# Mix stage and up-projection in one block: operand loads, differences and splits inside the last mix tiles; rows loaded ahead of weight pieces in the down-projection

## The chip, the core and the metric

The kernel runs on one core of one Trainium2 chip. The metric is the device time of one execution in microseconds (us); smaller is better. All data is float32. Matrix products are made as three products of a high and a low part (hi*hi, hi*lo, lo*hi), where the high part is the operand rounded to the type of TensorE's fast float32 mode and the low part is the remainder.

## What is computed

One layer of a streaming encoder over 2048 tokens of width 1024, cut to what matters:

```
h    = layer_norm(x)
q, k, v, u = split(h @ w_in)
mix  = concat([attention(q, k, v), conformer_conv(u)]) @ w_o
h1   = layer_norm(alpha * h + mix)
z    = causal_conv3(h1 @ w_up)                 # 2 * 2816 channels
act  = gelu(z[:, :2816]) * z[:, 2816:]
out  = layer_norm(alpha * h1 + act @ w_down)
```

## The kernel before

There are three stages, one after the other. Each is a block: every engine runs its own list of instructions, ordered by semaphores that are written out by hand, and the next block starts when all engines are through.

**Projection** (`phase_project`) is not touched.

**Mix stage** (`phase_mix`). 16 tiles of 128 tokens go through a software pipeline of five positions, `body(q, p, c, n, m)`: m is rotated and its convolution summed, n has its scores and softmax, c is projected with `w_o`, p gets its residual and layer norm, q is transposed and stored. Three more bodies drain the pipeline after tile 15 has been n (tiles count from 0). On VectorE (DVE) a body begins with `residual(p)` and ends with `row_norm(p)`: three one-column instructions (lines 111, 113, 115) and a `tensor_scalar` over the row (L1096). `affine(p)` on GpSimd (POOL) then multiplies by the gain and adds the bias (L877, L879). TensorE (PE) may write the projection of c into `m_y` only when `residual` of the tile before has read it (`after(pe, resid_ok, c.t)` in `project_attn`). `residual(p)` also waits until the row of two tiles before has left its buffer `m_r` (`h1_st`). The normed rows go to memory as rows (L770) and transposed (L774), both through SyncE's (SP) DMA queue, which also carries all loads.

**Feed-forward stage** (`phase_ffn`). The up-projection is Strassen's scheme in the Winograd form: 1024 tokens at a time (pass p), seven products of half-size operands, `Q1 Q6 Q7 Q5 Q2 Q4 Q3`. A step makes one pair of 128-channel tiles for 1024 tokens: seven products of 12 matmuls. The right operands are the quarters of the transposed rows, B11, B12, B21, B22, and their differences T1 = B12 - B11, T2 = B22 - T1, T3 = T2 - B11, T4 = B21 - T2. They are loaded from memory into `u_stage` and `u_gy` (L1569), cast to the high part on ScalarE (ACT, `right_hi`, L1726) and subtracted to the low part on DVE (`right_lo`, L1873), once per pass. In `first`, the differences of pass 0 are made on DVE (L1965, L1970, L1972, L1975). The left operands are loaded per step (L1565), summed on POOL (L1648 to L1654) and split on ACT (L1716) and DVE (L1869).

The down-projection is the same scheme again: 7 phases of 8 units, 33 matmuls each (L2307). Unit u needs 128 token rows of the gated product, loaded by `load_rows(u)`, cast by `rows_hi` (ACT, L1517) and split by `rows_lo` (DVE, L1533). During phase ph the weights of phase ph+1 are prepared in 11 pieces, two per unit in the first four (`SHARE`): `load_piece`, `weight_sum` (POOL, L1507 and L1509), `piece_hi` (ACT, L1529), `piece_lo` (DVE, L1538). Five buffers `d_wd_raw` go round. On ACT, unit u does in this order: `rows_hi(u+1)` (not for u = 0), `take(u-1)`, then the pieces of its share; DVE likewise.

Of the kernel before, what the change touches and what calls it, by code (L numbers as in the profile page):

```python
# [22 lines left out]
F32 = mybir.dt.float32  # L23
# [597 lines left out]
def phase_mix(nc, trig_scr, par, con, w_o, ln_g, ln_b, h_scr, qkv_scr, conv_scr, h1_scr, h1T_scr):  # L621
    ctx = ExitStack()
    with ctx:
        def sb(name, shape, dt=F32):
            return ctx.enter_context(nc.sbuf_tensor(name, shape, dt))

        def ps(name, shape):
            return ctx.enter_context(nc.psum_tensor(name, shape, F32))

        used = []  # L630

        def sem(name):
            used.append(ctx.enter_context(nc.semaphore(name)))
            return used[-1]

        wo_hi = sb("m_wo_hi", [P, KT, D], F32R)
        wo_lo = sb("m_wo_lo", [P, KT, D], F32R)
        mix_hi = sb("m_mix_hi", [P, 2, KT, P], F32R)
        mix_lo = sb("m_mix_lo", [P, 2, KT, P], F32R)
        ident, ones = sb("m_ident", [P, P]), sb("m_ones", [P, P])  # L640
        turned = sb("m_turned", [P, 2, 5, P])
        eps, one = sb("m_eps", [P, 1]), sb("m_one", [P, 1])
        cg, cb, sink = sb("m_cg", [P, CT]), sb("m_cb", [P, CT]), sb("m_sink", [P, NKV, GROUPS])
        g_bc, b_bc = sb("m_g", [P, D]), sb("m_b", [P, D])
        cos, sin = sb("m_cos", [P, SEQ]), sb("m_sin", [P, SEQ])
        wo_raw = sb("m_wo_raw", [P, WO_SLOTS, D])
        qk_in = sb("m_qk_in", [P, 2, 5, P])
        v_in = sb("m_v_in", [P, 2, CHUNK + P])
        conv_in = sb("m_conv_in", [P, 2, CT, P])
        h_in = sb("m_h_in", [P, 2, D])  # L650
        qk_cos, qk_sin = sb("m_qk_cos", [P, 5, P]), sb("m_qk_sin", [P, 5, P])
        qr, kr = sb("m_qr", [P, CHUNKS, 4 * CHUNK]), sb("m_kr", [P, CHUNK + P])
        vw = sb("m_vw", [P, CHUNKS, P])
        prob = sb("m_prob", [P, NKV, GROUPS, KEYS + 1])
        top, peak = sb("m_top", [P, NKV, GROUPS]), sb("m_peak", [P, NKV, GROUPS])
# [46 lines left out]
        block = ctx.enter_context(nc.Block())  # L702

        q_rows = qkv_scr.rearrange("q p t -> (q p) t")
        half = ROT // 2

        def load_wo(eng, k):

# [1672 lines left out]
```

## Time and profile before

| what | us |
|---|---|
| median of 3 runs | 2026.48 |
| lowest, highest | 2026.16, 2028.93 |
| the profiled execution, its own time | 2024.93 |
| its span, first to last instruction | 2023.2 |
| PE busy | 1871.2 |
| DVE busy | 1555.3 |
| ACT busy, POOL busy | 977.7, 961.6 |

PE is the busiest engine with 92% of the span; the mean granted clock of TensorE over the span is 0.968 of full speed. Times in the rows count from the start of the span. A timeline row gives start, duration, engine, line, operation, output<-input, shapes, count, and in brackets the idle time of the engine before it and what ended it.

### The profile page before, as it was taken

The page shows a single profiled execution, that of the slowest core. Times are in us where ns is not written, and L with a number is a line of the kernel's source. Part 1 is how long each engine was busy: PE and PEld are TensorE (multiplying, and loading weights), DVE is VectorE, ACT ScalarE, POOL GpSimd, SP SyncE. Part 2 cuts the span into 40 slices and gives each one's busy share as a digit, 9 for nine tenths or more (in the row PEclk, how much of TensorE's full clock was granted, in tenths as well). Part 3 has the DMA queues.
Part 4 walks back from the last instruction along what each step waited for, and adds up shares of the span by engine and source line. Part 5 has one row for each costly group of instructions (what it writes and reads, how often), then busy time and mean ns, then how long its engine had stood idle before and what let it go on. Part 6 is the DMA issues. An engine that isn't in the chain of part 4 may idle for free.

```text
span 2023.2 us, 27605 instructions
## 1 busy us (share of the span) xinstructions
PE 1871.2 (92%) x8520; PEld 1528.4 (76%) x8520; DVE 1555.3 (77%) x1874; ACT 977.7 (48%) x1508; POOL 961.6 (48%) x694
## 2 busy tenths in 40 slices
PE   3899999489999489999999899999999799999997
PEld 3788888367777368888888678888888688788886
DVE  8779878479998488888878888888888644666786
ACT  4555556367777344444444544444444333232454
POOL 5587788246666335444444554444443555520000
PEclk8999999699999699999999999999999899999999
DMA  7311211634443432322322332222224544387553
GB/s 253 146 36 64 71 57 47 195 108 149 139 144 106 170 124 96 120 95 97 116 93 102 109 108 101 104 105 102 104 104 143 173 130 147 122 276 237 176 185 137
DMA packets 200043, 257.48 MB, mean 127 GB/s; under 512 B 12208, under 2 KB 131504, under 8 KB 199472
## 3 DMA queue, kind: packets, MB, share of 16 engines
q1 hardware_dynamic: 191456, 233.24, 35.2%
q10 hardware_dynamic: 8528, 23.51, 3.2%
q8 instruction: 30, 0.49, 0.1%
q14 instruction: 29, 0.24, 0.0%
HBM read 172.10 MB, written 84.61 MB: 127 GB/s over the span
## 4 chain that ended last, share of the span: by engine, by line
PE 35%; issue 14%; POOL 8%; DVE 4%; DMA 3%; ACT 1%; SPq 0%; POOLq 0%; ACTq 0%; DVEq 0%
PE u_mm L2078 19%; PE d_y L2307 16%; DMA d_wd_raw<-w_down 2%; POOL u_w_sum L1650 1%; POOL u_w_sum L1648 1%; DVE u_r_lo L1873 1%; POOL d_wd_raw L1509 1%; POOL u_s L1664 1%; POOL u_s L1667 1%; DVE d_a_lo L1533 1%; POOL d_wd_raw L1507 1%; POOL u_s L1661 1%; DVE u_w_lo L1869 1%; ACT d_a_hi L1517 0%; DMA d_a_raw<-gated_scr 0%
## 5 line engine op out<-in xcount | busy, mean ns | idle before, releaser
L2078 PE MATMUL u_mm<-u_r_hi,u_w_hi 128*128 128x512 f32 x1232 | 484.0, 393 | 42.1 <-DVE u_r_lo L1873 26.2
L2078 PE MATMUL u_mm<-u_r_lo,u_w_hi 128*128 128x512 f32 x1232 | 482.3, 391 | 0.0
L2078 PE MATMUL u_mm<-u_r_hi,u_w_lo 128*128 128x512 f32 x1232 | 482.2, 391 | 0.0
L2078 PEld LDWEIGHTS u_mm<-u_r_hi,u_w_hi 128*128 128x128 f32 x1232 | 233.2, 189 | 95.3 <-issue 39.8
L2078 PEld LDWEIGHTS u_mm<-u_r_lo,u_w_hi 128*128 128x128 f32 x1232 | 233.4, 189 | 48.5
L2078 PEld LDWEIGHTS u_mm<-u_r_hi,u_w_lo 128*128 128x128 f32 x1232 | 233.0, 189 | 48.7
L2307 PE MATMUL d_y<-d_wd_hi,d_a_hi 128*128 128x512 f32 x616 | 243.4, 395 | 14.3 <-DVE d_a_lo L1533 13.9
L2307 PE MATMUL d_y<-d_wd_lo,d_a_hi 128*128 128x512 f32 x616 | 242.2, 393 | 0.0
L2307 PE MATMUL d_y<-d_wd_hi,d_a_lo 128*128 128x512 f32 x616 | 241.9, 393 | 0.0
L1904 DVE SCALAR_TENSOR_TENSOR u_y<-u_z,u_taps,u_y 128x1024 f32<-128x1024 f32 x176 | 222.6, 1287 | 15.1 <-DVE u_z L1918 3.5
L524 DVE SCALAR_TENSOR_TENSOR a_acc<-a_glu,a_taps,a_acc 128x2048 f32<-128x2048 f32 x84 | 197.9, 2356 | 15.2 <-DVE a_acc L524 14.4
L1648 POOL TENSOR_TENSOR u_w_sum<-u_w_raw 128x512 f32<-128x512 f32 x44 | 58.9, 1339 | 305.3 <-DMA u_w_raw<-w_up 286.5
L1869 DVE TENSOR_TENSOR u_w_lo<-u_w_raw,u_w_hi 128x512 fp32r<-128x512 f32 x132 | 147.3, 1117 | 43.3 <-ACT u_w_hi L1716 43.2
L545 PE MATMUL a_mm<-a_hT_hi,a_w_hi 128*128 128x512 f32 (+1 forms) x448 | 176.6, 394 | 0.0
L413 POOL TENSOR_TENSOR a_gb<-a_gb,a_spare 128x512 f32<-128x512 f32 x128 | 161.3, 1309 | 30.9 <-ACT a_spare L311 30.9
L545 PE MATMUL a_mm<-a_hT_hi,a_w_lo 128*128 128x512 f32 (+1 forms) x448 | 175.4, 391 | 0.0
L545 PE MATMUL a_mm<-a_hT_lo,a_w_hi 128*128 128x512 f32 (+1 forms) x448 | 175.3, 391 | 0.0
L1716 ACT CAST u_w_hi<-u_w_sum 128x512 fp32r<-128x512 f32 x176 | 105.1, 620 | 111.9 <-POOL u_w_sum L1650 44.2
L2307 PEld LDWEIGHTS d_y<-d_wd_hi,d_a_hi 128*128 128x128 f32 x616 | 117.1, 190 | 41.5 <-DVE d_a_lo L1533 15.6
L1869 DVE TENSOR_TENSOR u_w_lo<-u_w_sum,u_w_hi 128x512 fp32r<-128x512 f32 x176 | 137.9, 793 | 9.2 <-ACT u_w_hi L1716 3.7
L2307 PEld LDWEIGHTS d_y<-d_wd_hi,d_a_lo 128*128 128x128 f32 x616 | 117.2, 190 | 24.7
L2307 PEld LDWEIGHTS d_y<-d_wd_lo,d_a_hi 128*128 128x128 f32 x616 | 117.3, 190 | 24.4
(214 smaller groups left out, 3420.5 us busy)
## 6 DMA issues: line engine op xcount, KB each, us to landing
u_w_raw<-w_up SPq DMA_DIRECT2D x44, 1024.0 KB, 5.0
d_a_raw<-gated_scr SPq DMA_DIRECT2D x56, 704.0 KB, 5.1
gated_scr<-u_s SPq DMA_DIRECT2D x88, 256.0 KB, 2.0
d_wd_raw<-w_down SPq DMA_DIRECT2D x88, 256.0 KB, 5.1
gated_scr<-u_gy SPq DMA_DIRECT2D x44, 256.0 KB, 2.1
a_xs<-x SPq DMA_DIRECT2D x16, 512.0 KB, 4.6
m_h_in<-h_scr SPq DMA_DIRECT2D x16, 512.0 KB, 4.0
h_scr<-m_r SPq DMA_DIRECT2D x16, 512.0 KB, 4.7
```

Of the source, the lines that this page charges most:

```text
L413: nc.gpsimd.tensor_tensor(p, p, prod[:, i % 2, :], ALU.add).then_inc(part_ok, 1)
L524: v = nc.vector.scalar_tensor_tensor(out=acc[:], in0=src, scalar=tap_of(j, k), in1=acc[:], op0=ALU.mult, op1=ALU.add)
L545: last = nc.tensor.matmul(mm[bank][:], w[:, slot, k, :], h[:, k, rhs_at], start=(k == 0 and w is w_hi and h is hT_hi), stop=(k == KT - 1 a ...
L1507: nc.gpsimd.tensor_tensor(t, t, wd_hi[:, old, k, :].bitcast(F32), ALU.subtract).then_inc(wsum_ok, 1)
L1509: nc.gpsimd.tensor_tensor(t, t, wd_lo[:, old, k, :].bitcast(F32), ALU.subtract).then_inc(wfin_ok, 1)
L1533: nc.vector.tensor_tensor(a_lo[:, u % 2, :, :], a_raw[:, u % 2, :, :], a_hi[:, u % 2, :, :].bitcast(F32), ALU.subtract).then_inc(alo_ok, 1)
L1648: nc.gpsimd.tensor_tensor(w_sum[:, 0, :, :], a21, raw_of(Q4), ALU.add).then_inc(sum_ok, 1)
L1716: nc.scalar.copy(w_hi[:, s, :, :], left_of(s)).then_inc(whi_ok, 1)
L1869: nc.vector.tensor_tensor(w_lo[:, s, :, :], left_of(s), w_hi[:, s, :, :].bitcast(F32), ALU.subtract).then_inc(wlo_ok, 1)
L1904: v = nc.vector.scalar_tensor_tensor(out=y[:, m, :], in0=z[:, m, k:k + SPAN], scalar=tap(st, m, k), in1=y[:, m, :], op0=ALU.mult, op1=ALU.add)
L2078: last = nc.tensor.matmul(mm[BANK[s]][:], w[:, s, k, :], h[:, s, k, :], start=(s in FRESH and k == 0 and w is w_hi and h is r_hi), stop=(k ...
L2307: m = nc.tensor.matmul(dy[u % BANKS][:], a[:, u % 2, k, :], w[:, ph % 2, k, :], start=(k == 0 and a is a_hi and w is wd_hi), stop=(k == HA ...
```

## The change

`phase_mix` and `phase_ffn` become one function and one block, `phase_rest`. No engine meets another between the two stages any more, and the semaphores of the mix stage are not cleared in between. All buffers of the up-projection are laid over those of the mix stage in an order that lets them be written as the mix buffers die: the form of Q1 and Q6 lie over those parts of the `w_o` operands that tile 15's `project_rest` reads last, Q7 and Q5 over the rest, Q2 over the mix operands, Q4 over `m_h_in` and the gain, Q3 over `m_r` and `m_h1T`. Each engine's list goes on past tile 15:

- SP issues the four 1 MB loads of pass 0's operands, the taps and the bias between the bodies of tile 12 and tile 13, the first left operand after tile 14's body, B22 a second time after two more bodies, and the second left operand after the last transposed row is stored.
- POOL makes three left sums, then T1, T2 and T3 (2048 columns each) right after its body of tile 15.
- DVE and ACT mix the splits of the seven right operands and of the first left operands with the residuals, norms and copies of tiles 14 and 15. `row_norm` of tiles 13, 14 and 15 applies gain and bias itself (two `scalar_tensor_tensor` of 1024 columns on DVE), and POOL's `affine` is left out for them.
- PE makes Q1, Q6, then transposes row tile 14, then Q7, Q5, Q2, transposes row tile 15, then Q4, Q3.

In the down-projection the rows of unit 3 and two more weight pieces are loaded before the last store of the up-projection, the casts and splits of a phase's pieces begin one unit later (`SHARE[i - 1]` in unit i), and `take` of units 0 and 1 has new waits, because `d_total` now lies elsewhere. High and low part of the down weights share one buffer.

The core of the diff:

```diff
+            sp.wait_ge(wo_lo_ok, KT)
+            for s in range(2):
+                sp.wait_ge(h1T_st[s], 16 * (NT // 4 + 1))
+            load_b(stage[:, 0, :, :], 0, 0, 0, b11_ld)
+            load_b(stage[:, 1, :, :], 0, 0, 1, b12_ld)
+            load_b(stage[:, 2, :, :], 0, 1, 1, b22_ld)
+            load_b(spare, 0, 1, 0, b21_ld)
+            sp.dma_start(taps[:, :, :], ...).then_inc(con_ld, 16)
+            sp.dma_start(bias[:], ...).then_inc(con_ld, 16)
+            for t in (NT - 3, NT - 2):
+                body(at(t - 3), at(t - 2), at(t), at(t + 2), at(t + 3))
+            sp.wait_ge(cos_ok, NT)
+            sp.wait_ge(sin_qk_ok, 2 * NT)
+            load_w(0)
...
+            left_sums(Step(0, 0, 0), 3)                       # POOL, after body of tile 15
+            nc.gpsimd.tensor_tensor(stage[:, 1, :, :], stage[:, 1, :, :], stage[:, 0, :, :], ALU.subtract).then_inc(diff_ok, 1)
+            nc.gpsimd.tensor_tensor(stage[:, 2, :, :], stage[:, 2, :, :], stage[:, 1, :, :], ALU.subtract).then_inc(diff_ok, 1)
+            nc.gpsimd.tensor_tensor(early, stage[:, 2, :, :]..., stage[:, 0, :, :]..., ALU.subtract).then_inc(diff_ok, 1)
...
+            residual(c)                                       # DVE, c is tile 14, d is tile 15
+            log_gate(d)
+            attn_lo(d)
+            weights_lo(opening, Q1)
+            swish(d)
+            conv_lo(d)
+            row_stats(c)
+            weights_lo(opening, Q6)
+            weights_lo(opening, Q7)
+            row_norm(c)
+            for s in (Q5, Q2, Q4):
+                weights_lo(opening, s)
+            right_lo(0, Q1)
+            right_lo(0, Q6)
+            residual(d)
+            right_lo(0, Q7)
+            row_stats(d)
+            right_lo(0, Q5)
+            make_u2(opening)
+            row_norm(d)
+            make_u3(opening)
+            right_lo(0, Q2)
+            make_c22(opening)
+            nc.vector.tensor_tensor(spare, spare, stage[:, 2, :, :], ALU.subtract).then_inc(t4_ok, 1)
+            weights_lo(opening, Q3)
+            right_lo(0, Q4)
+            make_c21(opening)
+            for s in range(2):
+                dve.wait_ge(h1T_st[s], 16 * (NT // 2 + 1))
+            right_lo(0, Q3)
...
+            product(opening, Q1, 0)                           # PE
+            product(opening, Q6, 0)
+            turn_rows(c)
+            product(opening, Q7, 0)
+            product(opening, Q5, 0)
+            product(opening, Q2, 0)
+            turn_rows(d)
+            product(opening, Q4, 0)
+            product(opening, Q3, 0)
...
-                if ph < P3:
-                    for k in SHARE[i]:
+                if ph < P3 and i:
+                    for k in SHARE[i - 1]:
                         piece_hi(act, ph + 1, k)
...
+                    if u == 0:
+                        act.wait_ge(act_ok, 2 * FT)
+                    if u == 1:
+                        act.wait_ge(odd_st, 32 * FT)
+                        act.wait_ge(s4_ok, FT)
                     nc.scalar.copy(total[:, LO, i, FIRST], dy[u % BANKS][:]).then_inc(dp1_ok, 1)
```

## Rows read from the trace of the kernel before

**Rows 1.** The page, part 2: tenths of PE busy in 40 slices, clock below.

```profile
PE   3899999489999489999999899999999799999997
PEclk8999999699999699999999999999999899999999
```

**Rows 2.** Busy time by stretch: start:end, length, PE, PEld, DVE, ACT, POOL, PEclk, DMA.

```profile
655.00:667.00 12.00, 11.93 (x56) 9.76 (x56) 5.11 (x12) 2.56 (x6) 3.90 (x2) 1.00 0.26 89
667.00:697.00 30.00, 3.22 (x17) 2.45 (x17) 7.80 (x12) 8.59 (x11) 11.21 (x7) 0.56 0.58 205
697.00:733.20 36.20, 23.77 (x85) 18.16 (x86) 31.84 (x24) 15.63 (x16) 10.04 (x5) 0.85 0.23 83
752.40:771.50 19.10, 19.10 (x86) 15.83 (x85) 16.50 (x19) 8.87 (x13) 14.53 (x9) 1.00 0.27 97
```

**Rows 3.** Timeline of PE at the boundary of the two stages.

```profile
655.07 0.73 PE L1245 MATMUL m_y<-m_wo_hi,m_mix_hi 128*128 128x512 f32 x2 [1.21 <-ACT m_mix_hi L927]
697.01 0.77 PE L2078 MATMUL u_mm<-u_r_hi,u_w_hi 128*128 128x512 f32 x1 [16.77 <-DVE u_r_lo L1873]
```

**Rows 4.** Timeline of PE in the down-projection: the three stalls and the spacing after one.

```profile
1593.22 0.80 PE L2307 MATMUL d_y<-d_wd_hi,d_a_hi 128*128 128x512 f32 x1 [5.88 <-DVE d_a_lo L1533]
1597.22 0.63 PE L2307 MATMUL d_y<-d_wd_hi,d_a_hi 128*128 128x512 f32 x1
1598.51 0.63 PE L2307 MATMUL d_y<-d_wd_hi,d_a_hi 128*128 128x512 f32 x1
1608.06 0.79 PE L2307 MATMUL d_y<-d_wd_hi,d_a_hi 128*128 128x512 f32 x1 [4.36 <-DVE d_a_lo L1533]
1741.69 0.50 PE L2307 MATMUL d_y<-d_wd_hi,d_a_hi 128*128 128x512 f32 x1 [3.38 <-DVE d_a_lo L1533]
```

**Rows 5.** Timeline of DVE and POOL around the last mix tiles.

```profile
620.19 0.81 DVE L1096 TENSOR_SCALAR m_r<-m_r,m_mv,m_l 128x1024 f32<-128x1024 f32 x1
649.51 0.15 DVE L1088 TENSOR_SCALAR m_l<-m_mv 128x1 f32<-128x1 f32 x1
652.78 1.22 DVE L1056 SCALAR_TENSOR_TENSOR m_r<-m_h_in,m_y 128x1024 f32<-128x1024 f32 x1 [1.22 <-PE m_y L1245]
694.57 2.29 DVE L1873 TENSOR_TENSOR u_r_lo<-u_stage,u_r_hi 128x2048 fp32r<-128x2048 f32 x1 [2.77 <-ACT u_r_hi L1726]
643.52 0.46 POOL L873 TENSOR_TENSOR m_square_sum<-m_square_pair 128x128 f32<-128x128 f32 x1
```

**Rows 6.** Timeline of POOL and DVE where both read SBUF; line 113: min/median/max ns.

```profile
1116.62 4.63 POOL L1691 TENSOR_TENSOR u_stage<-u_stage 128x2048 f32<-128x2048 f32 x1 [1.32 <-DVE u_edge L1916]
1120.17 3.22 DVE L1873 TENSOR_TENSOR u_r_lo<-u_stage,u_r_hi 128x2048 fp32r<-128x2048 f32 x1 [1.21 <-ACT u_r_hi L1726]
L113 DVE SCALAR_TENSOR_TENSOR m_l<-m_l x16: 159/1214/1223, 440.6 to 672.2; 128x1 f32<-128x1 f32 x16
```

**Rows 7.** Timeline of SP's queue and of DVE where the loads go in.

```profile
610.25 0.42 SPq L770 DMA_DIRECT2D h_scr<-m_r  x1
621.05 1.22 DVE L1056 SCALAR_TENSOR_TENSOR m_r<-m_h_in,m_y 128x1024 f32<-128x1024 f32 x1
685.44 0.46 SPq L1569 DMA_DIRECT2D u_stage<-h1T_scr  x1
691.89 0.60 SPq L1604 DMA_DIRECT2D u_bias<-par  x1
```

**Rows 8.** DMA issues between 684 and 705: count, KB each, median us to landing.

```profile
u_stage<-h1T_scr SPq DMA_DIRECT2D x3, 1024.0 KB, 11.5
u_w_raw<-w_up SPq DMA_DIRECT2D x1, 1024.0 KB, 4.9
u_bias<-par SPq DMA_DIRECT2D x1, 22.0 KB, 9.3
```

**Rows 9.** Timeline of ACT between the first units of the down-projection.

```profile
1587.04 1.14 ACT L1529 CAST d_wd_hi<-d_wd_raw 128x512 fp32r<-128x512 f32 x2
1588.09 1.36 ACT L1517 CAST d_a_hi<-d_a_raw 128x1408 fp32r<-128x1408 f32 x1
```

More of the change, by code:

```diff
@@ L829, in _, with step @@
+            def step(st):
+                left_sums(st.plus(1))
+                gated_sums(st.plus(-1))
             for s in range(2):
@@ new lines, in final @@
+            def final(st):
+                prev = st.plus(-1)
+                weights_hi(st, Q3)
+                tap_g(prev)
+                keep_p1(st)
+                gelu(prev)
+                act.wait_ge(mm_ok, made(st, Q6))
+                rows_hi(act, 0)
+                act.wait_ge(mm_ok, made(st, Q7))
+                rows_hi(act, 1)
+                for k in range(5):
+                    piece_hi(act, P1, k)
+                take_c11(st)
+                for k in range(5, HALF):
+                    piece_hi(act, P1, k)
+                tap_v(st)
+                tap_g(st)
+                gelu(st)
@@ new lines, in _ @@
+            out_T(d)
+            act.wait_ge(h1_st[1], 16 * (NT // 2 + 1))
+            act.wait_ge(h1_st[0], 16 * (NT // 2 + 1))
+            right_hi(0, Q3)
+            for s in (Q1, Q6, Q7, Q5, Q2, Q4):
+                weights_hi(opening.plus(1), s)
+            tap_v(opening)
+            step(Step(0, 1, 0))
+            with act.Fori(1, HALF - 1) as n:
+                step(Step(n, 0, 0))
+                step(Step(n, 1, 0))
+            step(Step(HALF - 1, 0, 0))
+            turn(Step(HALF - 1, 1, 0))
@@ L1204, in _, with product @@
+            turn(Step(HALF - 1, 1, 0))
+            again(Step(HALF, 0, 1))
+            with dve.Fori(HALF, FT - 1) as n:
+                step(Step(n, 1, 1))
+                step(Step(n, 2, 1))
+            final(Step(FT - 1, 1, 1))
         @block.tensor
         def _(pe):
+            def product(st, s, fresh):
+                pe.wait_ge(wlo_ok, split(st, s))
+                if fresh is not None:
+                    pe.wait_ge(rlo_ok, 7 * fresh + FORMS[fresh].index(s) + 1)
+                if s in FRESH:
+                    after(pe, {Q1: c11_ok, Q6: u2_ok, Q7: c21_ok, Q5: c12_ok}[s], st.i)
+                else:
+                    pe.wait_ge({Q2: p1_ok, Q4: u3_ok, Q3: c22_ok}[s], st.i + 1)
+                for k in range(HK):
+                    for w, part in ((w_hi, HI_PART), (w_hi, LO_PART), (w_lo, HI_PART)):
+                        last = nc.tensor.matmul(mm[BANK[s]][:], w[:, s, k, :], forms[:, POS[s], part, k, :],
+                                                start=(s in FRESH and k == 0 and w is w_hi and part == HI_PART),
+                                                stop=(k == HK - 1 and w is w_lo), skip_group_check=s not in FRESH)
+                last.then_inc(mm_ok, 1)
@@ L1206, in _, with step @@
+            def step(st, fresh=None):
+                for s in st.order():
+                    product(st, s, fresh)
             pe.wait_ge(con_ld, 16 * 5)
@@ L2274, in _ @@
                     rows_lo(dve, u + 1)
-                if ph < P3:
-                    for k in SHARE[i]:
+                if ph < P3 and i:
+                    for k in SHARE[i - 1]:
                         piece_lo(dve, ph + 1, k)
```

1482 lines of the change are left out of this document (713 added, 769 removed).

## The prediction, made before the changed kernel was built or run

> **What bounds the kernel now.** I read the page's slices first: PE is full nearly everywhere, and the granted clock is full (2.4 GHz) except at three dips [rows 1]. So only places where PE stands still, or restarts at the low clock, can give anything. The busy time by stretch then shows the boundary of the two stages. The last `w_o` product ends at 667.1; in the 30 us after it PE is busy 3.2, at a granted clock of 0.56, and in the next 36.2 us, which hold the first step of the up-projection, it is busy 23.8, at 0.85. A later step takes 19.1 us with PE full [rows 2]. The timeline of PE shows Q1 starting at 697.01, released by the low part of its right operand [rows 3]. So 66.1 us pass between the last mix product and the second step (733.2), where 19.1 us of products and under 2 us of transposes are needed: about 45 us could be won at most. The third view is DVE in the same place: it is busy 31.8 of the 36.2 us [rows 2]. The opening is bound by DVE's splits and differences as much as by the loads ahead of them. The fourth is PE in the down-projection: three stalls of 5.9, 4.4 and 3.4 us, all released by `rows_lo` [rows 4].
>
> **The opening, if nothing held the engines up.** Until tile 15's products begin, everything stands as before. After them DVE has to do, in order, 8 instructions of 2048 columns (seven low parts and T4), 15 of 512 columns, a residual, two sets of statistics and two norms. With 2.21 us for each long one (the row's 2.29 less the overlap of neighbours [rows 5]), 0.6 for a short one, 1.2 for a residual, 1.8 for statistics and 3.0 for a norm with gain and bias, that is 17.7 + 9.0 + 1.2 + 3.6 + 6.0 = 37.5 us, where each long part also needs 1.8 us of ACT ahead of it. I laid the lists of all engines out with these durations. Q1 then starts at 668.7, the last low part (Q3's, which waits for tile 15's transposed row to land) ends about 697.5, and step 2 starts at 702.8: 30.3 us earlier than 733.2.
>
> **What POOL adds.** The differences T1 to T3 move from DVE to POOL, at 4.6 us each instead of 2.2 [rows 6], and they stand right before the moment at which DVE norms tile 13. The trace shows what that does. A split of 2.2 us that began at 1120.17 took 3.22, ending 2.1 us after POOL's 4.63 us difference had ended (1121.25): it waited for POOL. The one-column instruction L113 takes 159 ns alone and 1214 ns in the median of 16, whenever POOL adds two buffers at that moment [rows 6]. So a DVE instruction that reads SBUF as POOL does waits for the end of POOL's instruction, and where both wait, one DVE instruction slips in between two of POOL's. The Trainium skill says the same (SBUF — State Buffer, Who interferes with whom: an exclusive lock, and the second one to issue fully blocks). By that rule the change is hurt here, and the trace agrees with it.
>
> Priced: POOL ends its sums of tile 15 at 643.98 [rows 5], three left sums of 1.3 bring it to 647.9, three differences to 652.5, 657.2 and 662.1. DVE starts tile 13's variance at 649.51 [rows 5]; its norm is five locking instructions, of which one passes at 652.5 and one at 657.2, so the last three (0.2, 1.2, 1.2) follow at 662.1 and end at 664.7. `residual` of tile 14 stands behind it in DVE's list and ends at 665.9 instead of 654.0. `project_attn` of tile 15 waits for it: PE stands still from 653.9 to 666, restarts at the low clock (+2.5 us), and ends its mix products near 680.7 instead of 667.1. The hand layout gives then: Q1 at 681.3, Q5 done at 693.6, Q2 from 697.4 at the low clock, the last low part at 710.2 (37.5 us of DVE work after 665.9, and 6.8 us of waits for a left sum, for ACT's cast of T4 and for product Q4), Q3 done at 715.3, where step 2 begins; its left operand lands at 713 and its sums are made while Q1 runs. That is 17.8 us earlier than before. A stall of 0.6 us that followed goes too: **-18.4 us**. Bounds: -31 without the blocking, -13 with one more difference in the way.
>
> **What the loads add.** Between tile 12 and 13 SP now issues 4 MB plus taps and bias. The same six issues took 7.0 us from the first (685.44) to the end of the last (691.89 + 0.60) [rows 7]. Their data came in order: the left operand issued first landed in 4.9 us, the 22 KB of bias, issued last, took 9.3 [rows 8], to 701.2. Tile 10's row store, before issued at 610.25, comes at about 617 now, behind these loads: 4 MB from 609.7 at the 390 GB/s of that stretch, then 0.5 MB of tile 13's input, then the row, about 625. `residual` of tile 12, at 621.05 before [rows 7], waits for that store: 4 us late, and PE is full there, so the delay goes through. After its 4 us, PE may restart at the low clock (+2). Bounds: 0, if the store isn't held by the loads ahead of it, and +7. I take **+5 us**.
>
> The norms of the last tiles cost DVE 2.4 us instead of the 0.81 of L1096 [rows 5]; for tile 13 this is in the layout above, and POOL's 4.8 us per tile fall away on the path from norm to transpose (in the layout too). Clearing of semaphores, the meeting of the engines and the new table load (1.3 us, on ACT behind tile 14's copy) cost nothing beyond the layout: DVE's splits cover them, and if they did not, they would cost 1.3.
>
> **Down-projection.** Unit 2 began at 1593.22 after 5.88 us of standing still, because ACT did two weight pieces (1587.04) before `rows_hi(2)` (1588.09), and DVE likewise [rows 9]. With the pieces one unit later, `rows_hi(2)` comes at 1587.0, its split ends at 1590 or, behind a POOL sum, 1591.2, and unit 2 begins 2.5 us earlier. The restart still falls to 1.2 GHz: after the stall three matmuls took 1.29 us (1597.22 to 1598.51) [rows 4], 0.43 each against 0.228 (19.1/84 [rows 2]), and that kept for a dozen matmuls: 2.3 us. Unit 2 then ends at about 1600.6. The rows of unit 3 are loaded already and cast before pieces 2 and 3, so they are ready at 1594 and the stall of 4.36 goes with its restart (2.3). Unit 3 would end at 1608.1; before, it began at 1608.06 and ended at 1617.8: 9.7 us. The third stall (3.38 at 1741.69, and 1.5 for its restart) comes from rows waiting behind pieces that POOL hasn't summed; with pieces loaded one unit ahead of use ACT doesn't wait for them: 4.9 us. `take(1)` waits for the last store to land (about 1591), before anything needs its bank. The price of the longer hold of the five buffers is that SP's loads wait for the splits of the unit before, which two units of lead cover; without that cover a stall like the old ones comes back. Sum: **-14.6 us**, bounds -5 (only the first two shrink) and -17.
>
> **Sum.** -18.4 + 5 - 14.6 = -28.0 us. The profiled execution took 2024.93 us (span 2023.2, 1.7 around it), 1.5 below the median. Against its own time that gives 1996.9; against the median of 2026.48, 1998.5 us.
>
> **Rivals.**
> - *The lock costs little, or the loads do not hold the row store.* If DVE's norm of tile 13 passes between POOL's instructions, the opening brings 31 instead of 18.4: 1986; if the loads cost nothing as well, 1981. For it: a DVE instruction whose operand lies in PSUM is not held (residuals, copies of z), and most of the tail's short instructions are of that kind. Against: the norm's five all read SBUF.
> - *New waits in the tail and a smaller gain below.* The loads cost 7, one more wait on ACT (in-order casts, T4) costs 5, and in the down-projection only the first stalls shrink (-8): -18.4 + 5 + 7 - 8 = -14.4, so 2012. For it: every engine's list is now one chain through the tail, and DVE is at its limit there.
> - *Slower: TensorE stays at 1.2 GHz.* In the stretch between 667 and 697 the granted clock was 0.56 with PE mostly still [rows 2]. The new opening has five stalls of 2 to 12 us within 60 us. If the clock stays low from tile 15's products through the opening and the second step, 11 + 19 + 19 us of products take twice as long, of which 5 are counted above: +44, so 2042. It decides from a mean granted clock under about 0.7 over 650 to 740. Against: every restart in the trace is back at full clock after about 5 us of products.
> - *It does nothing.* If some engine still had to wait for all others (DVE's wait for tile 15's transposed row stands before the last split only), the opening would stay as it is, and the loads' 5 us would take part of the gain below: -10, 2016. Not likely.
>
> **Chances.** Forecast (1993 to 2006): 0.55. First rival (1980 to 1992): 0.22. Second (2007 to 2016): 0.13, the idle one 0.03. Slower: 0.04. The rest, within 0.2% of before, 0.03. The range 1982 to 2011 leaves out less than 2 in 10. A difference of 0.2% (4 us) is about what a measurement of this kernel can tell from none. Faster by more than that: 0.93; within: 0.03; slower: 0.04.
>
> **What would show it.** In the trace after: POOL's three 4.6 us instructions end near 662 plus the delay of the loads; the two `scalar_tensor_tensor` of tile 13 follow them and not the statistics; PE stands still for about 12 us before `project_attn` of tile 15; Q1 starts 9 to 13 us before its old 697.0 (15.7 earlier, less what the loads cost); no unit of the down-projection but the third waits over 1 us. If PE goes on into tile 15's products without a stall, the lock was priced wrongly; if `residual` of tile 12 begins on time, the loads were.

## The result, and the profile after

The changed kernel takes 2009.47 us in the median of 4 runs (2007.70 to 2010.80); the kernel before took 2026.32 us beside it (4 runs, 2025.25 to 2028.93). The ratio is 0.9919, 95% interval 0.9906 to 0.9931: 16.8 us faster, 0.8%. The forecast was 1998.5 us, or 28 us faster. The sign and the range 1982 to 2011 held, but 11 us of the gain are missing: the time lies outside the 1993 to 2006 that the prediction gave to its own account (0.55) and inside the 2007 to 2016 of its second rival (0.13). The profiled execution of the changed kernel, the slowest of the four, took 2010.80 us with a span of 2007.8 us, 15.4 less than the span before.

The page, part 2, of the changed kernel, tenths of PE busy in 40 slices and the clock below, to be read beside [rows 1]:

```profile
PE   4899999489999689999999799999999899989997
PEclk9999999689999889999999999999999999999999
```

The 4 of the fourteenth slice has become a 6, the fifteenth stays at 8, and the 36th falls from 9 to 8. The timeline of PE of the changed kernel names the places (start, us, operation, in brackets the idle time before it and what ended it):

```profile
628.43 1.19 PE L2042 MATMUL m_y<-m_wo_hi,m_mix_hi 128*128 128x512 f32 x2 [4.86 <-DVE m_r L1779]
671.81 1.19 PE L2042 MATMUL m_y<-m_wo_hi,m_mix_hi 128*128 128x512 f32 x2 [11.19 <-DVE m_r L1779]
686.71 0.70 PE L1994 MATMUL u_mm<-u_forms,u_w_hi 128*128 128x512 f32 x2 [0.89 <-DVE u_forms L1617]
715.79 0.70 PE L1994 MATMUL u_mm<-u_forms,u_w_hi 128*128 128x512 f32 x2 [3.03 <-issue]
720.02 0.81 PE L1994 MATMUL u_mm<-u_forms,u_w_hi 128*128 128x512 f32 x2
736.04 0.70 PE L1994 MATMUL u_mm<-u_forms,u_w_hi 128*128 128x512 f32 x2 [2.04 <-DVE u_z L1627]
1125.90 0.69 PE L1994 MATMUL u_mm<-u_forms,u_w_hi 128*128 128x512 f32 x2 [1.05 <-ACT u_z L1327]
1562.16 0.61 PE L2360 MATMUL d_y<-d_wd,d_a_hi 128*128 128x512 f32 x2
1570.66 0.73 PE L2360 MATMUL d_y<-d_wd,d_a_hi 128*128 128x512 f32 x2 [1.53 <-DVE d_wd L898]
1582.99 0.74 PE L2360 MATMUL d_y<-d_wd,d_a_hi 128*128 128x512 f32 x2 [3.88 <-DVE d_a_lo L893]
1782.11 1.22 PE L2360 MATMUL d_y<-d_wd,d_a_hi 128*128 128x512 f32 x2 [2.70 <-DVE d_a_lo L893]
1802.70 0.74 PE L2360 MATMUL d_y<-d_wd,d_a_hi 128*128 128x512 f32 x2 [1.77 <-DVE d_a_lo L893]
```

The first two rows are the two prices that the prediction put on the opening: tile 12's and tile 14's residual come late, and the restart runs at the low clock (two matmuls in 1.19 us; the granted clock was 0.50 in the 2.6 us behind each). Q1 starts at 686.71, 10.3 before its old 697.01 [rows 3]. Q3's twelve matmuls follow at 715.79, and the second step begins at 720.02, 13.2 before 733.20 [rows 2]. Then comes a stall that the prediction did not have (736.04, granted clock 0.68 in the 5.3 us behind it), and three in the fourth phase of the down-projection (1782 to 1803), where the kernel before ran full. Of the down-projection's old stalls [rows 4] only unit 2's is left, 3.88 instead of 5.88; unit 3 and unit 20 wait no more. Within unit 0 there is a new one of 1.53.

For the places in between, four rows of the kernel before: PE at the first pass's last step, PE at unit 0, and DVE taking the products of units 24 and 30:

```profile
1135.76 0.47 PE L2078 MATMUL u_mm<-u_r_hi,u_w_hi 128*128 128x512 f32 x1 [1.06 <-ACT u_z L1737]
1571.15 0.39 PE L2307 MATMUL d_y<-d_wd_hi,d_a_hi 128*128 128x512 f32 x1
1781.03 0.69 DVE L2215 TENSOR_TENSOR d_total<-d_total,d_y 128x512 f32<-128x512 f32 x1 [0.61 <-PE d_y L2307]
1825.91 0.69 DVE L2215 TENSOR_TENSOR d_total<-d_total,d_y 128x512 f32<-128x512 f32 x1 [1.28 <-PE d_y L2307]
```

and the last two in the changed kernel:

```profile
1757.00 0.69 DVE L2268 TENSOR_TENSOR d_total<-d_total,d_y 128x512 f32<-128x512 f32 x1 [4.39 <-PE d_y L2360]
1810.56 0.69 DVE L2268 TENSOR_TENSOR d_total<-d_total,d_y 128x512 f32<-128x512 f32 x1 [2.43 <-PE d_y L2360]
```

How far the changed kernel is ahead at each place, and what the prediction's sum gives there:

| place | before | after | ahead | predicted |
|---|---|---|---|---|
| second step begins | 733.20 | 720.02 | 13.2 | 12.8 |
| last step of the first pass | 1135.76 | 1125.90 | 9.9 | 13.4 |
| unit 0 | 1571.15 | 1562.16 | 9.0 | 13.4 |
| unit 24 taken | 1781.03 | 1757.00 | 24.0 | 28.0 |
| unit 30 taken | 1825.91 | 1810.56 | 15.4 | 28.0 |
| end of the span | 2023.2 | 2007.8 | 15.4 | 28.0 |

So the two large terms came as predicted: the opening with its loads (13.2 for 12.8) and the down-projection up to unit 24 (24.0 - 9.0 = 15.0 for 14.6). Each row compares one execution with one: at 600 us, where the two kernels still do the same, the changed one is already 0.7 us late (a transposed row is issued at 600.62 for 599.94), so differences under 1 us say little. The missing 12.6 us of span went in two places: between the second step and unit 0, where 0.6 more should have been won and 4.2 were lost, and in the fourth phase of the down-projection, where 8.7 were lost (24.0 to 15.4). Twice 0.4 go the other way.

**The new stall in the second step.** Timeline of SP, ACT and DVE of the changed kernel:

```profile
712.52 0.38 SPq L967 DMA_DIRECT2D u_w_raw<-w_up  x1
717.38 0.62 ACT L1303 CAST u_w_hi<-u_w_raw 128x512 fp32r<-128x512 f32 x1 [6.43 <-DMA u_w_raw<-w_up]
727.19 5.12 DVE L1648 SCALAR_TENSOR_TENSOR u_y<-u_z,u_taps,u_y 128x1024 f32<-128x1024 f32 x4
```

SP issues the second step's left operand only when all stores of the mix stage have landed, at 712.52. ACT stands still for 6.43 us for it, DVE splits it up to 727 and only then begins the four taps of the first step. `make_u2` and `make_u3`, which add up PE's products, stand behind them, and PE waits for the second.

**The new stalls in the fourth phase.** Timeline of SP and DVE of the changed kernel:

```profile
1763.86 9.00 SPq L853 DMA_DIRECT2D d_wd_raw<-w_down  x4
1772.90 0.91 SPq L2154 DMA_DIRECT2D d_h<-h_scr  x2
1772.08 0.68 DVE L2268 TENSOR_TENSOR d_total<-d_total,d_y 128x512 f32<-128x512 f32 x1
1779.29 1.22 DVE L2271 SCALAR_TENSOR_TENSOR d_total<-d_h,d_total 128x1024 f32<-128x1024 f32 x1 [6.54 <-DMA d_h<-h_scr]
```

SP's four issues of weight pieces take 9.00 us, because each waits for one of the five piece buffers (in the kernel before, four such issues took 3.81). The two loads of h1 stand behind them on SP and go out at 1772.90. DVE needs h1 at 1772.76, waits 6.54 us, and `rows_lo` of the next unit stands behind it and runs from 1780.43, so PE waits too. The same place in the kernel before, where the pieces were split one unit earlier:

```profile
1790.48 0.80 SPq L2106 DMA_DIRECT2D d_h<-h_scr  x2
1796.71 1.22 DVE L2218 SCALAR_TENSOR_TENSOR d_total<-d_h,d_total 128x1024 f32<-128x1024 f32 x1
```

There h1 is issued 6.2 us before DVE uses it, and nothing waits.

### The profile page after: what moved, and what is told of

It reads as the page before. It is cut to its first block, busy times and chain, and to the rows that moved or that the text cites. A ratio compares the mean times of both kernels' runs of the same rounds, so it can differ in the third digit from the quotient of the medians.

```text
span 2007.8 us, 27606 instructions
## 1 busy us (share of the span) xinstructions
PE 1871.0 (93%) x8520; PEld 1529.7 (76%) x8520; DVE 1572.8 (78%) x1874; ACT 975.4 (49%) x1508; POOL 968.3 (48%) x691
## 4 chain that ended last, share of the span: by engine, by line
PE 38%; issue 17%; DVE 11%; POOL 6%; ACT 3%; DMA 3%; SPq 1%; POOLq 0%; ACTq 0%; DVEq 0%
PE u_mm L1994 19%; PE d_y L2360 18%; POOL u_w_sum L1146 1%; POOL u_w_sum L1144 1%; DMA d_h<-h_scr 1%; POOL u_s L1164 1%; DVE u_w_lo L1608 1%; POOL u_s L1167 1%; DVE u_forms L1617 1%; DVE m_stat L1806 1%; POOL u_s L1161 1%; ACT m_ce L1481 1%; DVE m_top L1837 1%; PE m_y L2042 1%; DVE m_den L1850 1%
## 5 line engine op out<-in xcount | busy, mean ns | idle before, releaser
L1994 PE MATMUL u_mm<-u_forms,u_w_hi 128*128 128x512 f32 x2464 | 767.1, 393 | 24.2 <-issue 12.1
L1994 PEld LDWEIGHTS u_mm<-u_forms,u_w_hi 128*128 128x128 f32 x2464 | 466.3, 190 | 125.4 <-issue 22.3
L1994 PE MATMUL u_mm<-u_forms,u_w_lo 128*128 128x512 f32 x1232 | 483.0, 392 | 0.0
L2360 PE MATMUL d_y<-d_wd,d_a_hi 128*128 128x512 f32 x1232 | 382.5, 392 | 11.7 <-DVE d_a_lo L893 10.1
L2360 PEld LDWEIGHTS d_y<-d_wd,d_a_hi 128*128 128x128 f32 x1232 | 232.4, 189 | 62.4 <-DVE d_a_lo L893 11.8
L1994 PEld LDWEIGHTS u_mm<-u_forms,u_w_lo 128*128 128x128 f32 x1232 | 233.5, 190 | 49.2
L2360 PE MATMUL d_y<-d_wd,d_a_lo 128*128 128x512 f32 x616 | 240.7, 391 | 0.0
L893 DVE TENSOR_TENSOR d_a_lo<-d_a_raw,d_a_hi 128x1408 fp32r<-128x1408 f32 x56 | 100.4, 1793 | 46.6 <-ACT d_a_hi L877 46.3
L2360 PEld LDWEIGHTS d_y<-d_wd,d_a_lo 128*128 128x128 f32 x616 | 116.4, 189 | 24.1
L311 ACT ACTIVATE a_spare<-a_glu,a_taps 128x512 f32<-128x512 f32 x128 | 91.9, 724 | 72.1 <-POOL a_gb L413 71.3
```

What stands on the lines that cost most here:

```text
L311: nc.scalar.activation(dst, glu[:, j % 2, bass.ds(c * BLK + k, BLK)], ACT.Copy, scale=tap_of(j, k)).then_inc(prod_ok, 1)
L893: nc.vector.tensor_tensor(a_lo[:, u % 2, :, :], a_raw[:, u % 2, :, :], a_hi[:, u % 2, :, :].bitcast(F32), ALU.subtract).then_inc(alo_ok, 1)
L1994: last = nc.tensor.matmul(mm[BANK[s]][:], w[:, s, k, :], forms[:, POS[s], part, k, :], start=(s in FRESH and k == 0 and w is w_hi and part ...
L2360: m = nc.tensor.matmul(dy[u % BANKS][:], a[:, u % 2, k, :], wd[:, ph % 2, k, part, :], start=(k == 0 and a is a_hi and part == HI_PART), s ...
```

## The experiments

Times are medians; "the changed kernel" is 2009.47 us.

### The six loads behind tile 10's row store

```diff
-            (four load_b, taps, bias)
-            for t in (NT - 3, NT - 2):
-                body(at(t - 3), at(t - 2), at(t), at(t + 2), at(t + 3))
+            t = NT - 3
+            body(at(t - 3), at(t - 2), at(t), at(t + 2), at(t + 3))
+            (four load_b, taps, bias)
+            t = NT - 2
+            body(at(t - 3), at(t - 2), at(t), at(t + 2), at(t + 3))
```

> The changed kernel, but SP issues the four 1 MB loads of the right operand, the taps and the bias after its list for tile 13 (after tile 10's row store) and not ahead of it. Theory (the loads hold the row store, residual of tile 12 waits for it): the stall of 4.86 us of TensorE before tile 12's attention product goes, and with it the restart at the low clock; everything behind it comes 6 to 7 us earlier and stays so: 2002.8 us (2001 to 2005). Rival 1 (the queue has to move these 4 MB anyway, and they now hold tile 11's row store): the stall moves one tile on, 2008 to 2010. Rival 2 (the opening waits for the loads themselves, now later): POOL's first difference starts later than 650.7 + its three left sums, and the time is 2010 to 2014.

Measured: 2003.77 us (2001.55 to 2008.10, 4 runs), ratio to the kernel before 0.9887 [0.9864, 0.9911]; 5.7 less than the changed kernel. Timeline of DVE and PE, first of the changed kernel, then of this one:

```profile
627.06 1.22 DVE L1779 SCALAR_TENSOR_TENSOR m_r<-m_h_in,m_y 128x1024 f32<-128x1024 f32 x1 [5.39 <-DMA h_scr<-m_r]
```

```profile
622.54 1.22 DVE L1781 SCALAR_TENSOR_TENSOR m_r<-m_h_in,m_y 128x1024 f32<-128x1024 f32 x1
666.56 1.19 PE L2044 MATMUL m_y<-m_wo_hi,m_mix_hi 128*128 128x512 f32 x2 [11.21 <-DVE m_r L1781]
```

The wait of 5.39 us for the store is gone, PE's stall of 4.86 us with it, and the stall before tile 15 lies 5.25 us earlier. The loads did hold the row store, and they can be moved without harm: the rivals (the same wait one tile later, or POOL waiting for the operands) did not appear. The time is in the expected range.

### POOL's three differences left out

```diff
-            nc.gpsimd.tensor_tensor(stage[:, 1, :, :], stage[:, 1, :, :], stage[:, 0, :, :], ALU.subtract).then_inc(diff_ok, 1)
+            pool.sem_inc(diff_ok, 1)
```

and likewise for the other two; Q7's form is cast from `stage[:, 2]`. The product of these forms is therefore not the right one; all other work stays.

> The changed kernel without POOL's three differences of the first half (T1 to T3): the forms that need them are cast from the undifferenced buffers, so that part of the result is left out; casts, splits, products and loads stay. Theory (POOL's differences block DVE's norm of tile 13 and so hold residual of tile 14): the stall of 11.19 us before tile 15's attention product goes, to under 1 us, and Q1 of the up-projection comes 11 to 14 us earlier; the stall that DVE's late list causes in the second step stays; 1997 us (1995 to 2001). Rival 1 (DVE is simply behind with its own work there): the stall stays over 5 us, 2004 to 2009. Rival 2 (the gain is won at the stall and given back in the opening, where DVE's splits wait for ACT's casts and for tile 15's transposed row): the stall goes, but the second step begins less than 6 us earlier, 2003 to 2007.

Measured: 1999.83 us (1999.03 to 2002.14, 4 runs), ratio 0.9868 [0.9849, 0.9887]; 9.6 less than the changed kernel. Timeline of PE:

```profile
662.47 0.73 PE L2039 MATMUL m_y<-m_wo_hi,m_mix_hi 128*128 128x512 f32 x2 [1.20 <-ACT m_mix_hi L1444]
677.11 1.19 PE L1991 MATMUL u_mm<-u_forms,u_w_hi 128*128 128x512 f32 x2 [2.57 <-DVE u_forms L1614]
706.16 0.70 PE L1991 MATMUL u_mm<-u_forms,u_w_hi 128*128 128x512 f32 x2 [3.03 <-issue]
```

The stall of 11.19 us is 1.20, Q1 comes 9.6 us earlier, Q3 (706.16 for 715.79) too, and the end as well. So what the differences cost at the stall goes through to the end in full, and none of it is won back in the opening. By itself this run cannot tell POOL's blocking of DVE from the time of the differences; the next one can.

### POOL waits until DVE has normed tile 13

```diff
+            pool.wait_ge(h1_ok, NT - 2)
             pool.wait_ge(b11_ld, 16)
```

> The changed kernel, but POOL starts its first difference only when DVE has ended its norm of tile 13. Theory (what is blocked is DVE work on SBUF alone; residual of tile 14, the gate's log, the low part of the attention and the low part of the convolution read PSUM and pass): the stall of 11.2 us before tile 15's attention product falls under 1.5 us, but DVE's splits and statistics, all in SBUF, now wait for POOL's three differences, so that Q1 starts only 2 to 4 us earlier: 2006 us (2004 to 2008). Rival 1 (instructions with an operand in PSUM are held as well): a stall of 4 to 12 us stays before that product, 2009 to 2012. Rival 2 (POOL's differences hold DVE up nowhere but at the norm): 1998 to 2001, as without them.

Measured: 2003.16 us (2002.51 to 2005.66, 4 runs), ratio 0.9885 [0.9869, 0.9902]; 6.3 less than the changed kernel. Timeline of POOL and DVE:

```profile
660.47 4.60 POOL L1252 TENSOR_TENSOR u_stage<-u_stage 128x2048 f32<-128x2048 f32 x1 [5.57 <-DVE m_r L1828]
665.15 4.94 POOL L1255 TENSOR_TENSOR u_stage<-u_stage 128x2048 f32<-128x2048 f32 x1
660.31 1.21 DVE L1780 SCALAR_TENSOR_TENSOR m_r<-m_h_in,m_y 128x1024 f32<-128x1024 f32 x1
661.61 0.69 DVE L1870 SCALAR_TENSOR_TENSOR m_ce<-m_tps,m_ce 128x512 f32<-128x512 f32 x1
662.82 2.80 DVE L1609 TENSOR_TENSOR u_w_lo<-u_w_raw,u_w_hi 128x512 fp32r<-128x512 f32 x1
667.49 1.28 DVE L1807 BATCH_NORM_STATS2 m_stat<-m_r 128x6 f32<-128x512 f32 x2
669.15 0.15 DVE L1812 TENSOR_SCALAR m_l<-m_mv 128x1 f32<-128x1 f32 x1
```

While POOL's first difference runs (660.47 to 665.07), two DVE instructions with one operand in PSUM (`m_y`, `m_tps`) pass at their usual 1.21 and 0.69 us. The split of `u_w_raw`, both inputs in SBUF, takes 2.80 instead of 0.68 and ends at 665.6. Under the second difference the statistics pass unheld at 1.28 for two, though they read SBUF. So rival 1 is out, the stall is POOL's blocking, and the theory was too wide: what is held is an instruction with two inputs in SBUF, not every one that works there. The stall before tile 15's product is 1.20 us, but PE now waits 9.73 us for Q1's low part, and Q1 comes at 683.98, 2.7 earlier. The gain is larger than expected (2004 to 2008). A part of this is that the second step's stall went too: the left operand is issued at 709.38 instead of 712.52, and DVE begins the taps at 724.20 instead of 727.19. By the last step of the first pass (1122.04) the trace is 3.9 us ahead of the changed kernel's. The rest lies where the edit changes nothing, at units 0 and 2 above all: in the traces of the versions that leave that place alone, unit 0's wait is between nothing and 1.53 us, and unit 2's between 2.77 and 3.88.

### The three differences on DVE

```diff
+            nc.vector.tensor_tensor(stage[:, 1, :, :], stage[:, 1, :, :], stage[:, 0, :, :], ALU.subtract).then_inc(diff_ok, 1)
+            nc.vector.tensor_tensor(stage[:, 2, :, :], stage[:, 2, :, :], stage[:, 1, :, :], ALU.subtract).then_inc(diff_ok, 1)
             right_lo(0, Q1)
+            nc.vector.tensor_tensor(early, ...).then_inc(diff_ok, 1)
             right_lo(0, Q6)
```

and the three on POOL go.

> The changed kernel, but the three differences of the first half are DVE's, 2.2 us each, two ahead of Q1's low part and one ahead of Q6's. Theory (without POOL's differences the kernel took 9.6 us less, and DVE is the bound of the opening, so it pays its 6.6 us there): no stall before tile 15's attention product, the second step starts about 3 us earlier, 2006.5 us (2003 to 2009). Rival 1 (DVE waits for ACT's casts in that place anyway, and the differences fill the gaps): 2000 to 2002. Rival 2 (the differences delay Q1's low part and PE restarts more often): 2009 to 2014.

Measured: 2006.20 us (2001.19 to 2006.73, 4 runs), ratio 0.9897 [0.9881, 0.9914]; 3.3 less than the changed kernel, as its price of 6.6 us on DVE said (9.6 - 6.6 = 3.0). In its trace Q3 starts at 712.25, 3.5 earlier than in the changed kernel. That trace is of the fastest of the four executions; the other three took 2005.7 to 2006.7, and the interval of the ratio lies between 1 and 8 us under the changed kernel's 0.9919.

### The second step's left operand earlier

```diff
-            for t in (NT + 1, NT + 2):
-                body(at(t - 3), at(t - 2), at(t), at(t + 2), at(t + 3))
+            body(at(NT - 2), at(NT - 1), None, None, None)
+            store_row(at(NT - 1))
+            refill(Step(0, 0, 0), 1)
+            store_turned(at(NT - 1))
...
-            refill(Step(0, 0, 0), 1)
```

and ACT waits for tile 15's turned row before `tap_v` of the first step.

> The changed kernel, but SP issues the load of the second step's left operand as soon as its buffer is split (about 706), between tile 15's row store and its transposed store, and not after all stores have landed (712.5). Theory (the left operand lands at 717.4, DVE stands still for it and is then behind in the second step): it lands near 711, and the stall of 2.04 us at 736 goes with its restart: 2005.3 us (2004.5 to 2007). Rival 1 (DVE is behind in the second step because of its own work, the left operand only adds to its idle time): the stall stays, 2009. Rival 2 (the transposed row now lands 2 us later behind the 1 MB, and the last low part and so Q3 waits for it): the second step begins 1 to 2 us later, 2007 to 2010.

Measured: 2005.26 us (2003.53 to 2010.16, 4 runs), ratio 0.9899 [0.9876, 0.9922]; 4.2 less. Timeline of SP, DVE and PE:

```profile
706.44 0.38 SPq L967 DMA_DIRECT2D u_w_raw<-w_up  x1
723.13 5.13 DVE L1650 SCALAR_TENSOR_TENSOR u_y<-u_z,u_taps,u_y 128x1024 f32<-128x1024 f32 x4
716.26 1.19 PE L1996 MATMUL u_mm<-u_forms,u_w_hi 128*128 128x512 f32 x2 [3.03 <-issue]
```

The load goes out 6.1 us earlier, DVE begins the taps 4.1 earlier, and PE then runs without a stall of over 0.5 us until the first pass's last step. Q3 starts at 716.26, 0.5 later than in the changed kernel, but Q1 (687.18 for 686.71) is late by the same 0.5, long before the load goes out, and the wait ahead of Q3 is the same 3.03 us: the store behind the 1 MB cost Q3 nothing, and rival 2 is out. The size of the gain is less sure than its place. The four executions reach from 2003.53 to 2010.16, and the interval of the ratio includes the changed kernel's 0.9919; in the trace 2.3 us are gained by the last step of the first pass (1123.57 for 1125.90).

### h1 ahead of the weight pieces

```diff
+                if ph == P4:
+                    load_h1(i, FIRST, (left_ok, i) if i else None)
                 if 1 < u and ph < P3:
                     for k in SHARE[i]:
                         load_piece(sp, ph + 1, k)
-                if ph == P4:
-                    load_h1(i, FIRST, (left_ok, i) if i else None)
```

> The changed kernel, but in the down-projection's fourth phase SP issues the unit's two loads of h1 ahead of the weight pieces and not behind them. Theory (SP stands at a piece whose buffer is not free yet, h1 is issued late behind it, DVE's take waits for h1 and rows_lo stands behind take): the three stalls of 2.70, 1.77 and 1.77 us at 1782, 1793 and 1803 go, with their restarts: 2002.5 us (2001.5 to 2004). Rival (the queue is full in that phase, 1 MB of pieces, 0.7 MB of rows and 0.5 MB of h1 per 7.5 us): the stalls stay or now wait for the pieces, 2008 to 2011.

Measured: 1999.61 us (1997.45 to 2003.49, 4 runs), ratio 0.9866 [0.9843, 0.9888]; 9.9 less, more than the expected 7 (2001.5 to 2004) and against 8.7 read from the table above. The two traces agree with the 8.7: their spans differ by 9.6, and 0.9 of that is there at unit 24 already, ahead of the edit. Busy time of the stretch 1755 to 1806, first of the changed kernel, then of this one (columns as in [rows 2]):

```profile
1755.00:1806.00 51.00, 44.76 (x188) 35.94 (x187) 24.23 (x27) 14.14 (x16) 10.34 (x9) 0.97 0.69 208
```

```profile
1755.00:1806.00 51.00, 51.00 (x227) 42.24 (x226) 35.97 (x32) 16.25 (x18) 16.86 (x10) 1.00 0.81 251
```

PE is full again, and 251 GB/s are moved where the changed kernel moved 208: the queue had room, SP's order did not use it. The rival is out.

### The down-projection's part alone

The kernel before, with the down-projection's lines of the change and nothing else.

> The kernel before with the change's down-projection part alone: rows of unit 3 and the pieces of the second unit loaded ahead of the turn, and in ACT's and DVE's lists each unit's weight pieces one unit later. Two stages stay apart as before. Theory (the stalls of units 2, 3 and 20 shrink by what the prediction says, 14.6 us, but the longer hold of the five piece buffers makes SP stand ahead of h1 in the fourth phase and gives 7 us back, and unit 0's last piece comes late, 1 to 2 us): 2020 us (2018 to 2022), with three stalls of 1.5 to 3 us in the fourth phase. Rival (the part gains its 14.6 us by itself, and it is the opening that disturbs it in the changed kernel): 2010 to 2014, no stall in the fourth phase.

Measured: 2019.90 us (2018.76 to 2020.64, 5 runs) beside 2026.68 for the kernel before, ratio 0.9964 [0.9950, 0.9978]: 6.8 less. Timeline of PE, the three longest stalls in the down-projection:

```profile
1593.19 0.80 PE L2313 MATMUL d_y<-d_wd_hi,d_a_hi 128*128 128x512 f32 x1 [2.74 <-DVE d_a_lo L1533]
1792.42 0.50 PE L2313 MATMUL d_y<-d_wd_hi,d_a_hi 128*128 128x512 f32 x1 [3.02 <-DVE d_a_lo L1533]
1803.60 0.50 PE L2313 MATMUL d_y<-d_wd_hi,d_a_hi 128*128 128x512 f32 x1 [3.41 <-DVE d_a_lo L1533]
```

The stalls of the fourth phase come with this part, whatever the opening does. The rival, a full 14.6 us from this part, is out. That leaves 10 of the 16.8 us for the stages above. The expectation also had unit 0's last piece late by 1 to 2 us; unit 0 waits 0.18 us here.

### Four mends together

The three single mends above, and ACT's cast and DVE's split of unit 2's rows ahead of the last step's gate.

> The changed kernel with four mends at once: the six loads behind tile 10's row store, the second step's left operand loaded as soon as its buffer is free, h1 ahead of the weight pieces, and, new, ACT's cast and DVE's split of unit 2's rows ahead of the last step's gate (ACT: before the gelu; DVE: after the four taps). Theory (the causes are independent; alone they gave 5.7, 4.2 and 9.9 us, and the last stall before unit 2, 3.88 us with a restart of 2, goes as well): 1985 us (1983 to 1989), stalls left: 11.2 us before tile 15's attention product, the three of the opening and the middle turn. Rival (one gain eats another: with the work earlier the same loads collide elsewhere, or unit 2 then waits for POOL's sums): 1990 to 1998.

Measured: 1989.66 us (1986.82 to 1992.07, 4 runs), ratio 0.9810 [0.9794, 0.9827]; 19.8 less than the changed kernel. That is the sum of the three single ones (5.7 + 4.2 + 9.9 = 19.8); the fourth added nothing that can be seen, and the time is just outside the expected 1983 to 1989, where the rival's range begins. Timeline of ACT and PE:

```profile
1584.67 0.62 ACT L889 CAST d_wd<-d_wd_raw 128x512 fp32r<-128x512 f32 x1 [2.33 <-POOL d_wd_raw L869]
1589.12 0.74 PE L2366 MATMUL d_y<-d_wd,d_a_hi 128*128 128x512 f32 x2 [2.01 <-DVE d_a_lo L893]
```

Unit 2 no longer waits, but unit 4 does, 2.01 us: its rows are cast behind this weight piece in ACT's list, and POOL sums the piece late. PE could take unit 4 at 1587.1, some 14 us earlier than in the changed kernel (about 1601); POOL's first sum behind the last store's operands came only 6.4 earlier (1577.65 for 1584.05). This is the rival's mechanism, two units further on.

### The mended kernel with the differences elsewhere

> The kernel with the four mends, and POOL starts its first difference only when DVE has ended its norm of tile 13. Theory (the gain of 6.3 us that this gave alone is independent of the four, less the 4.2 us that it had in common with the earlier load, since its second step had no stall either): 1986.5 us (1984 to 1989). Rival (with the second step's left operand early, POOL's sums for it block DVE's last low parts): 1989 to 1992.

Measured: 1987.39 us (1984.64 to 1989.87, 5 runs) beside 2025.20 for the kernel before, ratio 0.9812 [0.9798, 0.9827]. The time is in the expected range, but the ratio is that of the four mends without it (0.9810), so a gain from POOL's waiting is not shown here. In the trace the stall of 11.19 us before tile 15's product is 1.20, and PE waits 9.72 us for Q1's low part instead.

> The kernel with the four mends, and the three differences of the first half on DVE, 2.2 us each. Theory (alone this began the second step 2 to 3 us earlier than the version that lets POOL wait, and lost it again at the stall of 2.06 us that the earlier load takes away): 1984.5 us (1982 to 1987), faster than the other by 1 to 4 us. Rival (DVE's own 6.6 us cost as much as POOL's blocking with POOL waiting): equal within 1 us.

Measured: 1984.54 us (1982.92 to 1986.03, 5 runs) beside 2025.20 for the kernel before, ratio 0.9798 [0.9783, 0.9812]: the fastest here, 2% under the kernel before, and as expected. Whether it beats the other one stays open: the medians are 2.9 us apart, but the intervals overlap, and the two profiled spans are 1983.7 and 1983.6 us.

## Why the prediction was right or wrong

**The opening, and POOL in it: right.** The layout, -17.8 of the term's -18.4, is to be read against everything shifted ahead of it. DVE's variance row of tile 13 stands at 656.27 for 649.51 [rows 5], 6.8 later; Q1 was due at 681.3 + 6.8 = 688.1 and came at 686.7; the second step was due at 715.3 + 6.8 = 722.1 and came at 720.0, 2.1 early. (715.3 is 17.9 before 733.20, not 17.8, and the 30.3 of the undisturbed layout is 30.4; nothing hangs on it.) That the opening and the loads together came within 0.4 us (13.2 for 12.8) is in part luck: the opening gave 2.1 more than laid out, the loads took 1.1 more, and 0.7 was lost before either. The blocking went as laid out in kind. Timeline of POOL and DVE of the changed kernel:

```profile
654.58 4.60 POOL L1251 TENSOR_TENSOR u_stage<-u_stage 128x2048 f32<-128x2048 f32 x1
663.88 5.57 POOL L1260 TENSOR_TENSOR u_z<-u_stage 128x2048 f32<-128x2048 f32 x1
656.27 0.15 DVE L1811 TENSOR_SCALAR m_l<-m_mv 128x1 f32<-128x1 f32 x1
659.41 4.37 DVE L115 SCALAR_TENSOR_TENSOR m_l<-m_l 128x1 f32<-128x1 f32 x1
663.82 1.28 DVE L1825 SCALAR_TENSOR_TENSOR m_r<-m_r,m_mv,m_g 128x1024 f32<-128x1024 f32 x1
665.14 5.40 DVE L1827 SCALAR_TENSOR_TENSOR m_r<-m_r,m_l,m_b 128x1024 f32<-128x1024 f32 x1
670.46 1.21 DVE L1779 SCALAR_TENSOR_TENSOR m_r<-m_h_in,m_y 128x1024 f32<-128x1024 f32 x1
```

The one-column `L115` takes 4.37 us. The prediction let one of the norm's five instructions pass each time that POOL changes instruction and had three follow the third difference. In the trace two pass at each change, and only the last of the five waits for the third difference. The residual's end, 671.7, is still within 1 us of 665.9 + 6.8, since the last of the five waits for the third difference either way. PE stood still for 11.19 us where "about 12" was promised. The first rival is out: without the differences the time falls by 9.6 us, and with POOL only made to wait the stall goes. The Trainium skill (SBUF — State Buffer, Who interferes with whom) draws the line at two inputs in SBUF against a GpSimd instruction that reads SBUF, which is narrower than the prediction's rule; the version with POOL waiting agrees, with the split at 2.80 us and the statistics and PSUM readers unheld.

**The loads: right in kind, a little small.** Predicted +5 with bounds 0 and 7. The variance row is 6.8 late, of which 0.7 was there at 600 us, so the loads took 6.1; moved behind the row store they give back 5.7 us of the time. The step that was small is the residual's delay, put at 4: the row was awaited for 5.39 us and PE stood for 4.86, and the restart came on top.

**"A stall of 0.6 us that followed goes too": wrong.** The second step's stall did not go, it became 2.04 us with a restart. The hand layout had the left operand landed at 713 and its sums made while Q1 runs, and left open what DVE's list would do with that: the six splits stand ahead of the first step's taps and of `make_u2`. The landing itself came as laid out: 717.4, that is 2.6 us before the second step began, where the prediction had 2.3 (713 and 715.3). What failed is that so late a landing was taken to be harmless: DVE began the taps 4.1 us later than with the load issued early. In the place of -0.6 stands +3.3 (13.2 to 9.9) by the last step of the first pass; issued early, the load gives 4.2 us in the medians and 2.3 in the trace. Whether `make_u2` ahead of the splits would have done as well was not tried. A second, small loss, 0.9 between 1125.90 and unit 0, falls in the turn between the passes; the version with h1 first, the same up to there, loses 0.2, so most of it is this execution's own.

**The down-projection's gain: right to the place where it had been looked at.** From unit 0 to unit 24 the change gained 15.0 for 14.6. Within it unit 2's part was smaller (1.2 instead of 2.5 earlier against unit 0): PE stopped for 1.53 us at unit 0, for a weight piece that was split late. With h1 first, the same code up to there, unit 0's wait is 0.42 and unit 2 is 2.3 earlier (1582.07, with unit 0 at 1562.33), so the 2.5 nearly holds where that wait is short. Why its length differs from execution to execution is open.

**"SP's loads wait for the splits of the unit before, which two units of lead cover": the step that failed.** It holds for single pieces. In the fourth phase each piece of the next phase is the difference of two loaded ones, so four loads per unit go through five buffers, and SP stands for 9 us at them. The lead covered the pieces and the rows, but I had not looked at what else stands behind the pieces on SP's queue: h1, which DVE awaits in the same unit, ahead of `rows_lo`. It cost 8.7 us in the trace and 9.9 in time when mended: the term of -14.6 measured -6.4 from unit 0 to the end, and -6.8 in the version with this part alone. The prediction named the consequence ("without that cover a stall like the old ones comes back") and gave it no place in the sum, so that the total stayed in the range only by the width that the bound of -5 had given it. The prediction's own sign, that no unit but the third waits over 1 us, failed at four places: within unit 0, and three times in the fourth phase.

**The second rival** gave 2012 and was nearest in time, in part for another reason: it had the loads at 7 (they took 6.1) and a wait on ACT of 5 in the opening (the left operand's cost 2.3 to 4.2, by way of DVE), but in the down-projection it had only the first stalls shrinking, where all three shrank or went and the gain was given back later. The third rival, the clock staying low, did not appear: over the 650 to 740 that it was to be decided by the granted clock was 0.89, and 0.88 between 703.9 and 740. That last stretch of the changed kernel:

```profile
703.90:740.00 36.10, 29.37 (x113) 23.20 (x112) 26.02 (x27) 16.42 (x21) 10.80 (x8) 0.88 0.48 167
```

## What to carry to other kernels

When a step is given more lead, or its buffers are held longer, list everything that stands behind its loads on the same queue, and look at the phase where it has the most pieces, not the first one. Bandwidth does not give such a wait away: it was 208 GB/s with the stalls and 251 without. A large difference put on POOL is priced by the DVE instructions with two inputs in SBUF beside it. If one of these holds the tensor engine's next operand, try letting POOL wait until that instruction is through, or doing the same arithmetic on DVE in half the time: in the medians these gave 6.3 and 3.3 us on the changed kernel, but on the mended one 2.3 (not shown, the ratio is the same) and 5.1, so which is cheaper depends on what stands around it. And a trace is one execution: the same code gave a wait of 1.53 us within unit 0 and of 0.42.

## What the runs showed of the hardware that I had not expected

- With POOL's difference running, statistics over an SBUF row (1.28 us for two) and a one-column `TENSOR_SCALAR` (0.15 us) pass unheld, while a one-column instruction with two SBUF inputs takes 4.37 us. I had counted on all DVE work in SBUF being held.
- POOL is held as well: its third difference took 5.57 us for 4.60 where DVE's 1.28 us instruction had started 0.06 us ahead of it.
- After nearly the same wait (3.03 and 3.16 us) Q3's first two matmuls took 0.70 us in the changed kernel and 1.19 in the version with h1 first, whose code is the same up to there; the granted clock was 0.64 and 0.50 in the 4.2 us behind. What a restart costs differs from execution to execution.
